# Decode and prompt step of a two-layer convolutional trunk: the copies of old conv state in eight pieces on ScalarE's queue during the first out projection, and another stage order

## The reference, cut to what matters

```
for l in 0, 1:                                  # x: (tokens, 1024)
    h = rmsnorm(x, norm_g[l])
    a_val, a_gate, z_a, gb, gc, hb, z_b = split(h @ w_in[l])         # 7 x 1024 columns
    u = a_val * sigmoid(a_gate)                                      # group A, 8 heads x 128 channels
    ca, new_a = causal_dwconv(u, buf_a[l], conv_a_w[l])              # width 31
    y_a = silu(head_layernorm(ca + conv_a_b)) * silu(z_a)
    v = gc * hb                                                      # group B, 8 groups x 128 channels
    cb, new_b = causal_dwconv(v, buf_b[l], conv_b_w[l])              # width 3
    y_b = gb * cb * silu(z_b)
    x = x + concat(y_a, y_b) @ w_out[l]
return rmsnorm(x, final_g), new_a, new_b for prompt and decode
```

## Time and profile before

| | us |
|---|---|
| median of 3 runs | 1117.45 |
| lowest of the runs | 1116.68 |
| the profiled execution's own time | 1119.67 |
| its span on the slowest core (core 6) | 1118.1 |
| its spans on all cores | 1107.8 to 1118.1 |
| TensorE busy, core 6 | 1052.4 |
| VectorE busy, core 6 | 761.9 |
| ScalarE busy, core 6 | 633.6 |

### The profile page before, as it was taken

How to read it: one execution, slowest core, us unless ns; L and a number is a source line. 1 busy time by engine, 2 the same in 40 slices (tenths; PEclk the granted TensorE clock), 3 DMA queues, 4 the chain that set the end, 5 groups by cost and what they waited for, 6 DMA issues and landing times.

```text
span 1118.1 us, 20896 instructions; the slowest of 8 cores (1107.8 to 1118.1 us)
## 1 busy us (share of the span) xinstructions
PE 1052.4 (94%) x6692; PEld 523.5 (47%) x6818; DVE 761.9 (68%) x1524; ACT 633.6 (57%) x1031; POOL 314.7 (28%) x470
## 2 busy tenths in 40 slices
PE   6889997999999998999999999899999999789997
PEld 2344543545545543444454544454555454344464
DVE  3688876878888986133455898788888888533332
ACT  5855675776777664121161567677776856322232
POOL 6552232223322211222242222222222222113340
PEclk9999998999999999899999999999999999889998
DMA  9737758776776879544324765867687576931454
GB/s 232 180 91 111 114 124 127 124 125 115 135 120 111 135 139 199 117 149 149 121 66 90 120 103 126 129 132 129 107 149 132 81 121 125 187 78 67 149 159 126
DMA packets 185803, 142.44 MB, mean 127 GB/s; under 512 B 140000, under 2 KB 152160, under 8 KB 185632
## 3 DMA queue, kind: packets, MB, share of 16 engines
q0 software_dynamic: 34352, 54.97, 32.6%
q1 hardware_dynamic: 150912, 85.58, 31.1%
q10 hardware_dynamic: 432, 0.55, 0.1%
HBM read 149.08 MB, written 43.79 MB: 173 GB/s over the span
## 4 chain that ended last, share of the span: by engine, by line
PE 80%; DMA 12%; issue 2%; DVE 2%; POOL 2%; ACT 2%; SPq 0%; DVEq 0%; ACTq 0%; POOLq 0%
PE psb L720 49%; PE psb L970 27%; DMA big<-scr_c 2%; DMA wsl<-w_in_r 2%; DMA scr_c<-big 2%; DMA y_sb<-x_d 2%; DMA wsl<-w_out_r 2%; PE psb L1076 1%; PE psb L1077 1%; PE psb L1400 1%; DMA xst<-x_mid 1%; DMA y_fm<-xst 0%; POOL y_sb L1439 0%; DVE tmp L1250 0%; POOL toep L1480 0%
## 5 line engine op out<-in xcount | busy, mean ns | idle before, releaser
L720 PE MATMUL psb<-h_sb,wsl 128*128 128x512 bf16 (+1 forms) x2294 | 372.4, 310 | 15.3 <-DMA big<-scr_c 7.2
L720 PEld LDWEIGHTS psb<-h_sb,wsl 128*128 128x128 bf16 x2336 | 172.2, 99 | 188.5 <-issue 25.0
L1321 DVE TENSOR_TENSOR xst<-xst,psb 128x512 f32<-128x512 f32 (+2 forms) x80 | 45.0, 566 | 137.4 <-PE psb L720 118.4
L1050 ACT ACTIVATE toep<-wt_sb 32x512 bf16<-32x512 bf16 x192 | 119.8, 626 | 20.6 <-PE psb L1077 12.7
L758 ACT ACTIVATE tmp<-xst 128x1024 bf16<-128x1024 f32 (+2 forms) x44 | 38.5, 880 | 149.0 <-DVE xst L1321 137.2
L1250 DVE SCALAR_TENSOR_TENSOR tmp<-vbuf,cw_b_sb,tmp 128x512 f32<-128x512 bf16 (+1 forms) x160 | 107.7, 673 | 16.0 <-ACT tmp L1247 10.2
L970 PE MATMUL psb<-h_sb,wsl 128*128 128x512 bf16 x430 | 110.4, 379 | 2.0 <-ACT psb L978 0.8
L970 PE MATMUL psb<-xst,wsum 128*128 128x512 bf16 x433 | 109.4, 384 | 3.1 <-ACT tmp L1258 1.1
L708 POOL DMA_DIRECT2D wsl<-w_in_r x112 | 60.6, 545 | 166.9 <-PE psb L720 72.8
L970 PE MATMUL psb<-h_sb,wsum 128*128 128x512 bf16 x435 | 106.4, 379 | 1.1 <-DVE psb L991 0.4
L1043 POOL DMA_DIRECT2D wt_sb<-wt_d x64 | 34.9, 546 | 189.1 <-DVE toep L1054 89.6
(11 more groups left out here) (155 smaller groups left out, 1864.5 us busy)
## 6 DMA issues: line engine op xcount, KB each, us to landing
wsl<-w_in_r POOLq DMA_DIRECT2D x112, 256.0 KB, 5.6
scr_u<-u_sb SPq DMA_DIRECT2D x16, 704.0 KB, 6.5
up_sb<-scr_u SPq DMA_DIRECT2D x16, 704.0 KB, 7.3
scr_c<-big SPq DMA_DIRECT2D x16, 640.0 KB, 7.3
big<-scr_c SPq DMA_DIRECT2D x16, 640.0 KB, 5.9
wt_sb<-wt_d POOLq DMA_DIRECT2D x64, 128.0 KB, 3.7
xst<-x_d SPq DMA_DIRECT2D x16, 512.0 KB, 6.4
x_mid<-xst SPq DMA_DIRECT2D x16, 512.0 KB, 2.6
```

The lines of the kernel that those rows point to most:

```text
L720: ins = e.matmul(bank(v, n), lhsT=l_(), rhs=r_(), start=(first and i == 0), stop=(last and i == len(pairs) - 1))
L1050: act((lambda e, p=p, c=c: e.activation(out=toep[p, tp.slot, :].rearrange("p (m x) -> p m x", x=128)[:, :, 32 * c:32 * c + 32], in_=wt_sb[ ...
L1321: dve((lambda e: e.tensor_tensor(out=x.s(m, part), in0=x.s(m, part), in1=bank(v, n), op=ALU.add)), n, [v, xr], [xr], holds=x.hold(m), name ...
```

## The change

The copy is taken out of the place above. In layer 0's out projection, `out_final` issues it from ScalarE in eight pieces, for both layers: two pieces each time that a block of columns is done and the next begins, four times. A piece is four of the sixteen decode groups of one layer.

```
-        for part in order:
+        for n, part in enumerate(order):
             if part[1] == 0:
                 x_stage(l, part[0])
+            if not final and n >= 1:
+                for c in (2 * n - 2, 2 * n - 1):
+                    S.op("act", (lambda e, c=c: e.dma_start(out=oa_copy[c // 4, 4 * (c % 4):4 * (c % 4) + 4], in_=sa_orig[c // 4, 4 * (c % 4):4 * (c % 4) + 4, DS:WA - 1, :])),
+                         0.35, (), (), chan=f"copy{c}", dma=4.5, pkt=0.5, name="copy", after=[x_op[0]])
...
-        spdma((lambda e, l=l: e.dma_start(out=oa_copy[l], in_=sa_orig[l, :, DS:WA - 1, :])), 8.0, (), (), "copy", name="copy", pkt=0.5,
-              after=[cn_of[(l, 7, "op")]])
```

More of the change, by code:

```diff
@@ L47 @@
 ORDER = [
-    "C0 b0 a1 b1 C1 Z0 P2 C2 Z1 P3 a2 C3 P4 b2 P5 Z2 C4 a3 b3 P6 Z3 Z4 C5 C6 a4 P7 b4 C7 Z5 a5 b5 a6 b6 a7 Z6u0 b7u1 Z7up",
-    "C0 b0 a1 b1 C1 P2 C2 Z0 Z1 P3 Z2 a2 P4 C3 b2 P5 C4 a3 b3 P6 Z3 Z4 C5 a4 P7 C6 C7 b4 Z5 a5 b5 a6 b6 Z6u0 a7 b7u1 Z7up",
+    "C0 b0 a1 Z0 b1 C1 P2 C2 Z1 P3 a2 P4 C3 b2 Z2 a3 P5 C4 b3 Z3 P6 C5 a4 Z4 Z5 C6 b4 P7 C7 a5 b5 a6 b6 Z6u0 a7 b7u1 Z7up",
+    "C0 b0 a1 b1 C1 P2 Z0 C2 P3 Z1 a2 P4 C3 b2 Z2 P5 C4 P6 a3 b3 Z3 C5 C6 a4 Z4 Z5 P7 b4 Z6 a5 b5 C7 a6 b6u0 a7 b7u1 Z7up",
 ]
@@ L53 @@
 STEPSP = "P10 P50 P60 P30 P51 P11 P20 P61 P21 s P31 P70 P40 P71 P41"
-STEPSa = "P10 P11 P50 P60 P51 P20 P30 P70 P61 s P21 P40 P31 P71 P41"
-STEPSb = "P10 P50 P60 P11 P51 P61 P31 P21 P30 P20 P71 s P70 P41 P40"
+STEPSa = "P10 P11 P50 P60 P20 P51 P61 P30 P70 s P21 P40 P31 P71 P41"
+STEPSb = "P11 P50 P51 P21 P10 P61 P20 P60 P31 P30 P71 s P70 P41 P40"
 YPOOL, GPOOL, TACT, LSQ = False, False, 3, 1
@@ L58 @@
          [("toep", 2, 2), ("w", 6, 1), ("sum", 2, 2), ("big", 1, 2)]]
-OUTQ = (2, 0, 1, 3, 4)
+OUTQ = (0, 2, 1, 3, 4)
 FIRSTQ = (0, 1, 4, 2, 3)
-ZQ = (0, 4, 2, 3, 1)
+ZQ = (0, 4, 3, 2, 1)
 SDVE = (0, 1, 2, 3)
 C22B = False
-WK = ['P0 P1 P2 P3 P4 P5 P6 P7 a0 a2 a3 a4 a5 a6 a7 b6', 'P0 P1 P2 P3 P4 P5 P6 P7 a0 a1 a2 a3 a4 a5 a6 a7 b6 b7']
-BG = {"sd": -300, "p5b": 30, "co": 30, "y": 300, "hist": -300, "sz": -100, "wt": -30, "halo": -300, "sub": 30, "lsq": 100, "p": -30, "nrm": -300, "u2": -100, "c": -30, "p5": -30}
+WK = ['P0 P1 P2 P3 P4 P5 P6 a0 a2 a3 a4 a5 a6 a7 b4 b6 b7', 'P0 P1 P2 P3 P4 P5 P6 P7 a0 a1 a2 a3 a4 a5 a6 a7 b6 b7']
+BG = {"sd": -300, "p5b": 30, "co": 30, "y": 300, "hist": -300, "sz": -100, "halo": 30, "sdb": 100, "u2b": 100, "th": -30, "u2": 100, "sub": 30, "lsq": 100, "sb": 30, "p": 300, "s": -30, "tr": -30}
 CAPS = {"proj": 5, "conv": 2, "z": 1}
@@ L1119, in ln @@
         cn = cn_of[(l, j)] = V("big")
-        o = spdma((lambda e: e.dma_start(out=big[:, cn.slot].rearrange("p a t -> p (a t)"), in_=scr_c[l, j])), 1.5, [scrc_r[l][j]], [cn], "cn", pkt=0.18,
+        o = spdma((lambda e: e.dma_start(out=big[:, cn.slot].rearrange("p a t -> p (a t)"), in_=scr_c[l, j])), 2.2, [scrc_r[l][j]], [cn], "cn", pkt=0.18,
                   name=f"cn{j}")
@@ L1297, in x_stage @@
             spdma((lambda e, lo=lo, v=v: e.dma_start(out=xst[:, v.slot, 0:w], in_=src[128 * lo:128 * (lo + w)].rearrange("(p c) -> p c", c=w))),
[L1298 removed]
+                  1.9 * w / 1024, [] if l == 0 else [xmid_r[q][i]], x.res[2 * i:2 * i + 2] if q < 4 else x.res, f"xl{nx[0] % NX}",
                   pkt=0.172 if q < 4 else 0.09, holds=[v], after=x_late if l == 0 else (), name=f"xl{q}.{i}")
@@ L1308, in x_store @@
               name=f"xm{q}.{i}")
+    x_op = [None]
     def out_block(l, part, m, lhs, wres, homes, ys):
@@ L1320, in out_block @@
         xr = x.r(m, part)
-        dve((lambda e: e.tensor_tensor(out=x.s(m, part), in0=x.s(m, part), in1=bank(v, n), op=ALU.add)),
+        x_op[0] = dve((lambda e: e.tensor_tensor(out=x.s(m, part), in0=x.s(m, part), in1=bank(v, n), op=ALU.add)),
             n, [v, xr], [xr], holds=x.hold(m), name=f"x{q}.{m}")
```

## The result

The changed kernel takes 1100.96 us (median) against 1117.70 for the kernel before in the same comparison: a ratio of 0.985, 95% interval 0.9828 to 0.9872. Its profiled execution took 1101.54, with a span of 1100.0 on the slowest core. The forecast was 1097, range 1086 to 1110, with a change within 2% as the likeliest: both hold. How the gain is made up was forecast less well, and that is what the rest is about. Some executions of every kernel have a whole die at a lower clock and take longer; the ratios and intervals leave them out, the medians do not, so it is the ratios that are to be compared.

The account below looks back on a forecast made before the run. TensorE, busy 94% of the span, was taken as the bound: its work plus idle and slow-clock time. Terms summed to -26.6 us on core 6 and -19.7 on core 0 (1097.5); slowest core near 1098, less 0.65: 1097 us, range 1086 to 1110.

Parts of the forecast that it names:

- Step 1: Both layers: one more block in seven products instead of eight, 8 matmuls of 512 columns fewer, -1.7 us.
- Steps 2 and 3: Head 1's z blocks: more matmuls cover the read-back wait; on core 6 -7.6 us in layer 0, -4.2 in layer 1.
- Step 4: Start of layer 0's out projection: wait and slow clock of 9.0 us shrink to 1, -8.0 us on core 6.
- 6 stays: Bound at the start of layer 0's out projection: 6 us of the 9.0 of wait and slow clock remain.
- Step 5: Start of layer 1's out projection: first w_out wait goes, second remains; 9 of 16.1 us stay, -7.1 on core 6.
- Step 6: Eight copy pieces issued by ScalarE in layer 0's out projection: issues and transfers stay hidden, 0 us.
- the slow rival: Layer 0's out projection: pieces on four DMA engines take 24.2 to 36.8 us a pair, up to 1119 us; chance 0.06.
- Step 7: Rest of the order, both layers: moved blocks can meet new short waits, +2 us, bounds 0 and 7.6.
- the copy was not the cause: Both out projections: other bytes make loads late, so no gain there, 14 us on core 0: 1111 us; chance 0.12.
- the pieces hold up x: Layer 0's out projection: slow piece pairs delay x loads and stop TensorE, up to 1119 us; chance 0.06.
- a new wait takes the place of the old ones: A z block or conv meets a late transfer, 5 us idle and 3 of slow clock: 1105 us; chance 0.18.

Follow-up runs that it names:

- the first comparison: Four kernels on one chip: before without copies (0.9883), before with eight pieces on ScalarE (0.9927), after with the copy back on SyncE (0.9998), after without copies (0.9828).

## Why the prediction was right, and where it was not

The time fell by 16.7 us, with 20.5 forecast. On the two cores that I had worked out the sum came out: core 6 fell by 28.7 us (26.6 forecast), core 0 by 23.1 (19.7). Part of that is luck. All cores run the same program, and which is the slowest changes from execution to execution: in the runs of the kernel before that were made for the experiments each of the eight is it at least once, and in the changed kernel's it was core 1, 2 and 3. I had worked out the two that happened to wait most in one execution. The mean of the eight spans, 1113.7 before and 1095.2 after, fell by 18.4, and core 1, the slowest after, by 14.4. Of core 0's 23.1 us 5.2 lie in the first 160 us, of core 6's 28.7 4.0 in the tail (against 2.3 more at the start), where I had said that nothing changes. By steps (idle and clock together, from the stretches of each core; the start and the tail are not in it):

| step | forecast, core 6 | core 6 | core 1 | mean |
|---|---|---|---|---|
| 2, z block in layer 0 | -7.6 | -8.1 | -6.5 | -6.7 |
| 3, z block in layer 1 | -4.2 | -4.6 | -1.1 | -2.3 |
| 4, layer 0's out projection | -8.0 | -4.7 | -0.1 | -2.4 |
| 5, layer 1's out projection | -7.1 | -13.1 | -11.2 | -10.3 |
| 6 and 7, layer 1's beginning | 0 and +2 | +1.8 | +2.0 | +2.2 |

**Step 1 (-1.7).** The program has 8 matmuls fewer, as counted. Its effect in time was not isolated: the mean span fell by 18.4 us and mean idle and clock loss over the whole span by 17.6; only 0.8 are left between them, where 1.7 was forecast.

**Steps 2 and 3.** Right. With the copy back the z wait of layer 0 stays away and layer 1's stays short, so the order does it and not the copy's move. The transfers of head 1 in layer 0 also got faster: write and read-back took 19.4 us on core 6 and 19.3 on core 1 before, 14.5 and 17.1 after. On core 1, where the wait was 5.3, the 2.2 us of that do not reach and the added cover is needed; on core 6 the 4.9 would have removed the wait of 4.7 by themselves.

**Step 4 (1 us left).** Wrong, a term badly sized. The copy was indeed what made the old wait (0.1 us without it). But 4.4+2.2 us are left on the mean core (2.7 to 5.8 of idle time, where I had put 3 as the most), because the new order puts three w_in loads ahead of the w_out loads. I had counted the work between the release and the first use (15 us against 17) and the x loads, and not the loads on GpSimd's own queue ahead of the one that is read. The bound "6 stays" took it in.

**Step 5 (9 us left).** Too little forecast: 3.9+0.6 are left. On core 6 the loads between 945 and 972 us land after

```profile
DMA to landing us min/median/max: 6.9/7.4/8.2
```

where I took 10.5 for the last of them; the second wait, which I thought would stay at 6.4, is 2.0. In the old order without copies 4.8+1.6 are left, so 8.4 of the 10.3 us are the copy's absence. (Where I counted 28 products of 64 columns before, the rows have 32, which moves the estimate by 0.1 us.)

**Step 6 (0).** The first half of the slow rival's mechanism is real: a piece has four packets under way, not sixteen. But a pair takes 10 us and not 24.2 to 36.8, since the landings from which I scaled were those of a crowded time. x and the statistics stay hidden as I said; a pair's two issues took 1.5 us on ScalarE, the first pair's 1.9, against my 1.4 at most. But I asked only whether x is late, and not what else is issued behind the last pair: it is layer 1's weight load, about 1 us here and 8 in the old order.

**Step 7 (+2).** About right: what is new at layer 1's beginning, less the pieces' 1 us, and 1.4 us more between 200 and 410.

Two of the signs that I had named, besides step 4's, did not come as written. Layer 1's wait for w_out is 1.4 to 2.6 us over the cores and not 4 to 8. And between 200 and 435 us stand new waits just above 1 us, 1.1 on core 6 at 349 us and 1.2 on core 4 at 387, both for ScalarE: by the letter a sign of a wrong forecast, in size within step 7.

So step 4 gave 3.3 us less than forecast on core 6 and step 5 6.0 more, and the total was close partly because these work against each other. And the new order by itself has not been shown to save any time: with the copy in its old place it takes as long as the old order (0.9998), and the old order with the copy moved and spread is at 0.9872, not told apart from the whole change (0.985). What it wins at the two z blocks, 9.0 us on the mean core, it loses again, with the copy in its old place 7.3 of them at layer 0's out projection. Of the rivals, "the copy was not the cause" is refuted by leaving the copy out, and "the pieces hold up x" by the stretch from 462 to 562 us; "a new wait takes the place of the old ones" holds in part, in step 4.

## What to carry to other kernels

Before a load that an engine will wait for, count the bytes that stand ahead of it on every queue, and ask of each when it is first read: 0.26 MB of weights that are read 130 us later cost 1.8 us, about what the second half of the copy cost for as many bytes (5.4 us for 0.85 MB, so 1.7). A wait moves less than in proportion to these bytes until the slack is gone, and about one for one from there. And a transfer in the background should be cut with an outer count of 16: with 4, a load behind it landed 11.2 us after its issue, and with 16, 7.9.

## What the runs showed of the hardware that I had not expected

A semaphore that held an issue back for 7.8 us cost at most 1 us: the load issued before it landed only 1.3 us earlier (451.7 and 453.0 us on core 1), since both were behind the same backlog. With the copy back the same load was held for 15.4 us on core 5 and landed 1.8 us behind the one issued before it.

The clock also falls where TensorE has not stood still. On core 3 of the old order with pieces it is busy throughout this stretch and is granted 0.81, neither the 1.2 nor the 2.4 GHz level:

```profile
414.90:421.40 6.50, 6.50 (x41) 3.02 (x39) 4.85 (x9) 2.66 (x6) 0.53 (x1) 0.81 1.01 207
```

Such stretches of 3.5 to 8 us, and single ones of 15.1 us, stand in all four profiled executions of the first comparison, which ran on one chip, and in none of the ten others. Cores 0 and 1, 2 and 3, 4 and 5 show them in pairs (28.1, 54.3 and 15.1 us in all in this execution; none on 6 and 7). At 0.19 of the clock the largest of these sums is 10 us of loss, with no wait to show for it. The Trainium skill (TensorE: Matmul & The Clock Gate, section "Seeing it yourself") names a limiter of peak current that takes a whole die to 13/16 of the clock while several of its cores multiply densely. The level agrees (13/16 is 0.81); the extent does not, since here pairs of cores go down together (in this execution 2 and 3 ten times, 0 and 1 of the same die five times) and come back within 15 us. What sets it off, and whether it is that chip's own, was not tried.
